# Sample attention: index keys scored inside the projection, the choice begun in the prompt stage, value sets placed between key sets

## What is computed

```
branch A: I[t,s] = sum_h w[t,h] * relu(q_idx[t,h] . k_idx[s]); the 256 best keys per token are kept,
          attention over them (8 query heads, 2 key/value heads)
branch B: blocks of 256 keys; each query head takes its 3 best past blocks by q . mean(k) and its own block
          (8 query heads, 8 key/value heads)
x += (sigmoid(gate_a) * (o_a @ w_br_a) + sigmoid(gate_b) * (o_b @ w_br_b)) @ w_out
```

## Time and profile before

| | us |
|---|---|
| median of 3 runs | 1334.08 (1330.1 to 1346.03) |
| the profiled execution | 1337.45 |
| its span in the trace | 1335.8 |
| around the span | 1.65 |
| projection, up to the first product of the prompt stage | 0 to 216.8 |
| prompt stage, up to the first instruction of the sample stage | 216.8 to 343.3 |
| sample stage: index keys, rows | 343.3 to 400.5 |
| sample stage: B keys and A keys | 400.5 to 520.0 |
| sample stage: B values, rounds | 520.0 to 608.0 |
| sample stage: mask of the choice, A | 608.0 to 663.5 |

### The profile page before, as it was taken

The page is one execution under the profiler, slowest core; times in us unless marked ns, Lnnn a source line. Parts: engine busy times, 40 slices in busy tenths (PEclk is TensorE's granted clock), DMA queues, the critical chain, the costliest instruction groups (busy, mean ns, idle before and its releaser), DMA issues. The chain is left out here.

```text
span 1335.8 us, 14762 instructions
## 1 busy us (share of the span) xinstructions
PE 1011.8 (76%) x5665; PEld 589.9 (44%) x5665; DVE 521.7 (39%) x882; ACT 291.5 (22%) x443; POOL 184.4 (14%) x240
## 2 busy tenths in 40 slices
PE   5999998889679997556679999995077776776720
PEld 4544444667536563112469999452022222222200
DVE  2215885443216979996143330213211111111106
ACT  3112213443136665001100000111001101011102
POOL 4100000000333244331200000000300101011030
PEclk9999998985589999776779999997578889899975
DMA  7212205200377879991584320110299999999963
GB/s 274 80 64 79 81 13 207 83 1 1 95 284 288 342 276 364 383 391 59 179 284 116 95 72 13 48 79 9 82 369 368 376 379 371 372 376 377 367 249 148
DMA packets 149830, 270.20 MB, mean 202 GB/s; under 512 B 18320, under 2 KB 109856, under 8 KB 141584
## 3 DMA queue, kind: packets, MB, share of 16 engines
q1 hardware_dynamic: 126624, 155.59, 34.5%
q0 software_dynamic: 23152, 113.86, 22.6%
HBM read 240.31 MB, written 29.11 MB: 202 GB/s over the span
## 5 line engine op out<-in xcount | busy, mean ns | idle before, releaser
L1853 PE MATMUL bank<-w_gate_up,xT 128*64 128x512 f32 x512 | 131.9, 668 | 47.6 <-DMA w_gate_up<-in_w_e_up 30.8
L637 PE MATMUL bank<-w,hT 128*128 128x512 f32 (+1 forms) x384 | 162.3, 578 | 2.1 <-DMA w<-in_w_in 2.1
L971 PE MATMUL bank<-consts,ring 128*128 128x128 f32 x704 | 95.6, 289 | 20.3 <-ACT kT_s L1144 7.2
L637 PEld LDWEIGHTS bank<-w,hT 128*128 128x128 f32 x384 | 72.6, 194 | 82.4 <-issue 71.3
L971 PEld LDWEIGHTS bank<-consts,ring 128*128 128x128 f32 x704 | 80.6, 147 | 60.3 <-ACT kT_s L1144 34.6
L1144 ACT COPY kT_s<-bank 128x1024 f32<-128x1024 f32 x88 | 86.4, 1016 | 75.9 <-PE bank L971 66.7
L1853 PEld LDWEIGHTS bank<-w_gate_up,xT 128*64 128x64 f32 x512 | 38.9, 152 | 130.4 <-issue 86.0
L1440 PE MATMUL bank<-hT_hi,gate_w_hi 128*128 128x272 f32 x256 | 76.4, 298 | 14.2 <-DVE gate_w_lo L1540 14.2
L1081 PE MATMUL bank<-ring,kT_s 128*32 128x512 f32 (+1 forms) x512 | 56.5, 594 | 37.0 <-DMA ring<-in_cache_v_b,rows_b 29.8
L1440 PE MATMUL bank<-hT_hi,gate_w_lo 128*128 128x272 f32 x256 | 74.8, 292 | 0.0
L1440 PE MATMUL bank<-hT_lo,gate_w_hi 128*128 128x272 f32 x256 | 74.8, 292 | 0.0
(11 more groups left out here) (302 smaller groups left out, 1418.9 us busy)
## 6 DMA issues: line engine op xcount, KB each, us to landing
w_gate_up<-in_w_e_gate SPq DMA_DIRECT2D x64, 512.0 KB, 9.5
w_gate_up<-in_w_e_up SPq DMA_DIRECT2D x64, 512.0 KB, 9.7
w_down<-in_w_e_down SPq DMA_DIRECT2D x32, 1024.0 KB
w<-in_w_in SPq DMA_DIRECT2D x5, 2048.0 KB, 8.3
expert_rows<-zeros SPq DMA_DIRECT2D x17, 512.0 KB, 5.1
gate_w<-in_w_in SPq DMA_DIRECT2D x16, 512.0 KB
expert_rows<-y POOLq DMA_DIRECT2D x16, 512.0 KB, 6.9
w_o<-in_w_out SPq DMA_DIRECT2D x1, 4096.0 KB
```

Source lines behind the costliest of these rows:

```text
L637: last = nc.tensor.matmul(bank[:, n % 4, 0:WID[g]], s.hT[:, k, t * P:(t + 1) * P], w[:, gi % 2, k, 0:WID[g]], start=(k == 0), stop=(k == K ...
L971: last = nc.tensor.transpose(bank[:, u, e * P:(e + 1) * P], ring[:, slot, at:at + P], ident)
L1853: last = nc.tensor.matmul(bank[r, 2, :], xT[:, kk, r], wgu[:, u, part, k, :], start=(kk == 0), stop=(kk == KD - 1))
```

## The change

- The index keys (16 units, `gather_keys`) are gathered during the projection and turned, scored and brought into `row` by steps between items 12 and 28 (`turn_keys`, `score_keys`, `index_rows` on TensorE; `keep_keys`, `keep_row` on ScalarE; `index_keys` on DVE). The gather rows are computed at item 5. For this the projection uses two banks (n % 2) in place of four; its weights, tokens and normalised rows lie in the ring's memory. The query tiles q_a, q_b are filled at the end of the projection.
- The prompt stage runs 8 of the 32 rounds on DVE, a MAX8 after step 1, 5, 9, ..., a MATCH_REPLACE8 after step 3, 7, 11, ...; POOL issues the first two sets of B keys (8 units) at its start.
- The sample stage has 24 rounds. Its sets come in the order of `sample_sets`: the value sets of B stand between key sets. `turn_rows(0)` and six `weigh` calls stand between the key steps, with a buffer `wT` of their own. `spread` comes after the last value set of B.

```diff
+def sample_sets():
+    return [("b", 0, 0), ("b", 0, 1), ("b", 0, 2), ("b", 0, 3), ("b", 1, 0), ("b", 1, 1), ("vb", 0, 0),
+            ("b", 1, 2), ("vb", 0, 1), ("b", 1, 3), ("vb", 0, 2), ("a", 0, 0), ("vb", 0, 3), ("a", 0, 1),
+            ("vb", 1, 0), ("a", 1, 0), ("vb", 1, 1), ("a", 1, 1), ("vb", 1, 2), ("vb", 1, 3),
+            ("va", 0, 0), ("va", 0, 1), ("va", 1, 0), ("va", 1, 1)]
...
 # project, POOL
+                if n == IDX0 - 2:
+                    gather_keys(0)
+                    gather_keys(1)
+                for k in (2, 3):
+                    if n == KEY0 + 3 * (k - 2) + 2:
+                        gather_keys(k)
...
 # project, DVE
+                if n == TT:
+                    gathered_rows()
+                if n == IDX0 + 1:
+                    index_queries()
+                if n == IDX0 + 2:
+                    index_new()
+                if KEY0 < n <= ROW0 and (n - KEY0) % 3 == 0:
+                    index_keys((n - KEY0) // 3 - 1)
...
+            attention_queries()
+            dve.wait_ge(row_done, 5)
...
 # project, TensorE
-                if n >= 4:
-                    pe.wait_ge(nat_ready, n - 3)
+                if n >= 2:
+                    pe.wait_ge(nat_ready, n - 1)
...
+            def index_rows(c):
+                w = 512 if c < 4 else SR
+                pe.wait_ge(key_summed, 2 * len(KSTEPS))
...
+                if KEY0 <= n < ROW0:
+                    k, step = (n - KEY0) // 3, (n - KEY0) % 3
+                    if step < 2:
+                        turn_keys(k, step)
+                    else:
+                        score_keys(k)
+                if ROW0 <= n < ROW0 + 5:
+                    index_rows(n - ROW0)
...
 # prompt, POOL
+            for n, unit in enumerate([(*at, u) for at in sample_sets() for u in range(4)][0:NR]):
+                gather_unit(pool, s, runs, n, unit)
...
 # prompt, DVE, at the end of step m
+                if m < n and m % 2 == 1:
+                    if m % 4 == 1:
+                        link(nc_max(link, s.best8[:, :], s.row[:, :]))
+                    else:
+                        link(nc_replace(link, s.row[:, :], s.best8[:, :]))
...
 # sample
-    UNITS = [("i", g, f, u) for g in range(G) for f in range(2) for u in range(4)]
+    UNITS = [(*at, u) for at in sample_sets() for u in range(4)]
+    TURN_AT = {23: 0, 36: 1}
+    WEIGH_AT = {24: (0, 0), 28: (0, 1), 32: (0, 2), 34: (0, 3), 36: (1, 0), 38: (1, 1)}
...
+            for n in range(1, NS):
+                if n in TURN_AT:
+                    turn_rows(TURN_AT[n], n)
+                if n in WEIGH_AT:
+                    weigh(*WEIGH_AT[n])
+                turn(n)
+                scores(n - 1)
+            scores(NS - 1)
             weigh(1, 2)
+            weigh(1, 3)
+            pe.wait_ge(a_kept, NAR)
             spread(0)
             spread(1)
-            weigh(1, 3)
-            turn_rows(2)
+            turn_rows(2, NS)
...
 # sample, ScalarE
-                if n == NI + 5 * PAIRS:
+                if n == 20:
                     exps(0)
-                if n == NI + NBR * PAIRS + 4:
+                if n == 34:
                     exps(1)
+                if n + 1 in TURN_AT:
+                    keep_turned(TURN_AT[n + 1])
...
 # sample, DVE
             keep_b(0)
+            for r in range(1, NCK):
+                rounds(2)
                 keep_b(r)
+            mask(0)
+            keep_b(NCK)
+            normalise(0)
+            rounds(2)
+            keep_b(NCK + 1)
+            for r in range(NCK + 2, NBR):
+                rounds(3)
+                keep_b(r)
             mask(1)
-            rounds(3)
             normalise(1)
-            rounds(9)
+            rounds(4)
             outputs(0)
-            rounds(TOPK_S // 8 - 24)
+            rounds(TOPK_S // 8 - TP * PAIRS // 2 - 18)
```

More of the change, by code:

```diff
@@ L191, in sa @@
                 return attn.enter_context(nc.sbuf_tensor(name, shape, dt))
[L192 to L193 removed]
+            both = sa("oaT_obT", [P, 2, PAIRS * NTOK])
+            s.oaT, s.obT = (both[:, x, :].rearrange("p (j r) -> p j r", j=PAIRS) for x in range(2))
             with ExitStack() as samp:
@@ L213, in build @@
[L213 to L216, removed]
+                s.q_b, s.q_a = ss("q_b", [P, NB, PAIRS, 32]), ss("q_a", [P, NB, 32])
+                s.row, s.best8 = ss("row", [SR, PAST + SR]), ss("best8_s", [SR, 8])
+                s.ring = ss("ring", [P, NR, SLOT_B * QW])
+                s.lg_i = both[:, :, :].rearrange("p x n -> p (x n)")[:, 0:2 * (PAST + SR)]\
+                    .rearrange("p (g n) -> p g n", g=2)
@@ L244, in project @@
     ROUND0 = IDX0 + 1 + PAIRS
+    G = NB // 4
+    KSTEPS = [(g, f) for g in range(G) for f in range(2)]
+    KEY0 = IDX0 + 2
+    ROW0 = KEY0 + 3 * len(KSTEPS)
     with ExitStack() as ctx:
@@ L457, in index_relu, with keep_keys, keep_row @@
                     .then_inc(relu_done, 1)
+            def keep_keys(k, half):
+                act.wait_ge(key_done, 2 * k + half + 1)
+                if half == 0 and k >= 1:
+                    act.wait_ge(key_scored, k)
+                nc.scalar.copy(kTi[:, 2 * half:2 * half + 2, :], bank[:, 2:4, :]).then_inc(key_kept, 1)
+            def keep_row(c):
+                act.wait_ge(row_done, c + 1)
+                keys = s.row[:, 0:PAST].rearrange("r (f p j e) -> r f e j p", f=2, j=4, e=2)
+                nc.scalar.copy(keys[:, c // 2, c % 2, :, :],
+                               bank[0:SR, 2 + c % 2, :].rearrange("r (j p) -> r j p", j=4)).then_inc(row_kept, 1)
             square(0)
@@ L666, in index_scores, with spread_weights, new_index @@
                 last.then_inc(idx_done, 1)
+            def spread_weights():
+                pe.wait_ge(rot_ready, order[ITEMS.index(("kv", TP))] + 1)
+                for g in range(G):
+                    last = nc.tensor.matmul(bank[:, 2, g * H:(g + 1) * H], const(s, "spread", SR)[:, g * P:(g + 1) * P],
+                                            s.wi[0:SR, TP, :], start=True, stop=True)
+                last.then_inc(w_done, 1)
+            def new_index():
+                pe.wait_ge(q_ready, 1)
+                for b in range(NB):
+                    r = slice(b % 4 * 32, b % 4 * 32 + 32)
+                    last = nc.tensor.matmul(bank[r, 3, b // 4 * SR:(b // 4 + 1) * SR], q_i[0:HD, b, :],
+                                            s.kiT[0:HD, SEQ:NTOK], start=True, stop=True)
+                last.then_inc(new_done, 1)
@@ new lines, in turn_keys @@
+            def turn_keys(k, half):
+                if half:
+                    pe.wait_ge(key_kept, 2 * k + 1)
+                elif k >= 1:
+                    pe.wait_ge(key_summed, 2 * k)
+                else:
+                    pe.wait_ge(new_read, 1)
+                for u in (2 * half, 2 * half + 1):
+                    r = (4 * k + u) % 8
+                    pe.wait_ge(key_in[r], 16 * (k // 2 + 1))
+                    for e in range(4):
+                        last = nc.tensor.transpose(bank[:, 2 + u % 2, e * P:(e + 1) * P], kidx[:, r, e * P:(e + 1) * P],
+                                                   ident)
+                last.then_inc(key_done, 1)
```

403 lines of the change are left out of this document (200 added, 203 removed).

## The result

The changed kernel takes 1345.84 us (median of 20 runs, 1339.33 to 1353.32), the kernel before beside it 1333.24 (20 runs): ratio 1.010, 95% interval 1.0078 to 1.0121. It is one per cent slower, which the forecast (1336, within 2%) counts as no change. The profiled execution has a span of 1343.7 us, 7.9 more than before.

The account below looks back on a forecast made before the run. TensorE bounds the projection, a three-engine loop the prompt stage, TensorE then DMA the sample stage's keys and values. From 1337.45 us, projection +24, prompt stage +24 and sample stage -49 sum to -1: 1336 us, range 1312 to 1361.

Parts of the forecast that it names:

- 7.9 + 4.4 + 7.2 + 2 + 3: Projection: transposes 7.9, scorings 4.4, row products 7.2, short products of weights and new keys 2, wait at index_rows(0) 3.
- Prompt stage, +24 forecast: Prompt stage: sixteen half rounds on DVE add 20 us and a lower clock 4; growth 24, range 17 to 34.
- the replacing ones: Prompt stage: the eight replacing half rounds stick out of gaps by about one us or fit; 4 us taken.
- the clock's term: Prompt stage: with more waits TensorE's clock falls earlier, some 15 us earlier, slowing products; 4 us taken.
- Sample stage, -49 forecast: Sample stage, from its start S: goes from 320.3 to 271 us, a change of -49, range -62 to -33.
- the first weighing: Sample stage: first weighing of B values begins at S + 90, S being the stage's start.
- the mixed stretch: Sample stage, B values among key sets: two pairs 42, four pairs 75, last B set 16 us; end at S + 223.
- The check on the floor of the gathers: Sample stage: 75.5 MB left to gather take 191 us from about S + 20; S + 223 is 12 above it.
- the A end: Sample stage, first spread product to last copy: 55.5 less 5 to 6 for weighing and 2 for waiting, so 48 us.
- The clock rival: Mixed stretch: key steps at 1.2 GHz add 21 us, the prompt stage's clock 6 more; 1363 us, chance 0.18.
- The faster rival: Half rounds cost little (prompt stage's 24 become 6), mixed stretch at the DMA floor, 12 less; 1306 us, chance 0.12.
- The rival in which the choice rules: Sample stage: waits on DVE come to 40, spread starts at S + 225 or later; 1336 to 1346 us, chance 0.1.

Follow-up runs that it names:

- e7_two_banks: The kernel before with only the projection's products in two PSUM banks in place of four; 1332.53 us, ratio 0.9985 to the kernel before.
- e3_keys_first: The changed kernel with its sets in the old order, all key sets ahead of value sets, weighings behind all key steps; 1341.35 us, ratio 1.0096 to the kernel before.
- e1_gap: The changed kernel with the same 16 half rounds of the prompt stage after even steps instead of odd; 1321.20 us, ratio 0.9937 to the kernel before.
- e2_no_prompt_rounds: The changed kernel without half rounds in the prompt stage, all 32 rounds in the sample stage; 1350.96 us, ratio 1.0154 to the kernel before.
- c1_gap_rows: The changed kernel with half rounds after even steps and index-row products one item later; 1315.84 us, ratio 0.9861 to the kernel before.
- e9_gathers_later: The changed kernel with index-key gathers for the third and fourth step issued about two items later; 1339.06 us, ratio 1.0106 to the kernel before.

## Why the prediction was right

**Projection, +24 forecast, +27.2 measured.** The terms were 7.9 + 4.4 + 7.2 + 2 + 3; measured 8.7, 5.2, 7.9, 0.9 and 2.7. That TensorE has no slack there is shown by the doubled transposes (9.3 to 9.7 for 64), that the wait at `index_rows(0)` is real by moving it (2.3 to 4.5 back), and that two banks cost nothing in the kernel before by e7_two_banks. The excess goes with the idle time near 117 us and the slow products behind it: where it is absent, the changed projection ends at 237.8 and 238.6, +21 and +22. It depends on the chip or its conditions, and not on the code alone.

**Prompt stage, +24 forecast, +22.5 measured.** The MAX8 behind `normalise` were to cost 16, the replacing ones 4, the clock 4. Against the stage before, the seven waits for the copy grew by 15.6, TensorE's busy time by 3.6, and its other idle time by 3.3: term for term the forecast. Moving the MAX8 gave 23.0 back, in which the clock's part is contained; that the replacing ones cost anything isn't shown by itself. Against the same kernel without rounds the cost is 27, since the stage before was itself slowed: 126.4 at clock 0.76, and 4.0 less in e7_two_banks, whose prompt stage is the same code, at 0.83. So the clock's term, 4, would have missed against such a profile: it is 11.0 there (113.3 against 102.3). The zero gap and the copy that `turn_out` waits for the earlier trace rows were the right rows to read; DVE's idle share of 58% was not.

**Sample stage, -49 forecast, -41.9 measured.** `spread` came at S + 222.7 where S + 223 was forecast, but that is luck in the steps: the first weighing came at S + 78 and not S + 90, and the mixed stretch took as much longer, 144.6 and not 133. What the runs do show is how little the sum moves: in ten kernels (the changed one among them, two with another order), in all of which DVE had the choice ready and waited 8 to 13 us for `spread`, it lies at S + 220.7 to S + 226.2. The check on the floor of the gathers would explain that, but with a DMA share of 0.80 over the stretch it is an argument and not shown; no run changed the bytes or TensorE's work there. The choice, due at S + 195 to S + 209, was ready at S + 212.4, with 11.21 of waiting at `normalise(1)` (10 to 25 were named). What came on top was DVE's waiting for scores to copy (`keep_b`), 14.57 at 486.71 and 8.77 at 510.44; it left 10.4 and not 14 to 28 of slack. The value sets ahead of these key sets aren't the reason: in e3_keys_first, without them, the choice was ready at S + 213.3.

**The term that was mis-sized is the A end: 48 forecast, 55.6 measured.** The weighing of the last B values is gone from it: from the first `spread` product to the turn is 20.0, was 25.0. The 2 us for the second A value set were not gained: it is there in time, but the third is then waited for (2.05). And the step priced the rest at the clock of the earlier trace rows, and the clock took the gain back: the first turn 3.67 in place of 1.97, and the final products 7.76 from 663.45 to the last copy, before 4.8 (from 658.64). In the three kernels where the clock of this part was at 0.73 the same code took 47.6 to 47.8, the forecast size (e3_keys_first, at 0.75, took 49.5). Why it is 0.61 to 0.75 from kernel to kernel stays open.

The three large terms missed by +3.2, -1.5 and +7.1 us, 8.8 together, of which the A end is 7.6. The forecast also starts from a profiled execution 4.2 above the median of 20 runs of the kernel before (1337.45 against 1333.24): it is a ratio of 0.999, where 1.010 was measured.

**Rivals.** The clock rival (1363) needed key steps at the low level in the mixed stretch; its clock was 0.83 there and not low throughout. The trace does show a set behind a wait of 7.24 taking 4.99 (539.45). The Trainium skill's page "TensorE: Matmul & The Clock Gate", section "HAM oscillation — how this bites in real kernels", says that bursts shorter than the DMA waits between them start slow every time, and the trace agrees: a set without a wait ahead takes 3.62. Sets are slow behind waits shorter than themselves too: 5.34 behind 2.83 at 558.83. But the value sets had time for it, and the turns of key steps between them ran at 1.97, the full-clock time, but for the first after a wait. The faster rival (1306) had a cheap place for the half rounds as its condition; the change doesn't have it, and e1_gap does. The rival in which the choice rules is e2_no_prompt_rounds. The claim that without the prompt's rounds the choice "would come 38 later and rule" was right in kind; it came later by 29.7 at `spread`, since 10.4 of it was slack.

**Where the gain went.** The change took 42 us out of the sample stage. It paid 27 for index keys in a stage where TensorE is full, and 22 to 27 for rounds put where DVE's next work is due at once. Only the second was shown to be avoidable; avoiding it, with the row products one item later, makes c1_gap_rows 1.4% faster than the kernel before, and some 2.4% faster than the change (0.9861 / 1.010).

## What to carry to other kernels

An engine's idle share says nothing of a place: before putting work on it, look at the idle time ahead of the instruction that comes next, and who waits for that one. Eight instructions of 2.3 us cost 23 behind `normalise`, more than their own 18.5 because TensorE's clock was lower as well, and nothing that was seen one step later. Work moved into a stage whose bound engine is full is paid in full. The order of transfers gained nothing here: keys first or mixed, `spread` came within 3 us of the same time.

## What the runs showed of the hardware that was not expected

- The same instruction sequence ran with granted clocks of 0.72 to 0.89 in the prompt stage, 134.5 to 118.8 us, and of 0.61 to 0.73 at the A end, 56.4 to 47.6. Terms of such stages carry that much by themselves.
- TensorE and ScalarE stood still for 3.1 to 3.7 and some 5 us at one place of the projection, in eight profiles of eight on some chips and in none of four on two others. What holds them up stays open; that no event of the core releases them is what the rows show.
- A stage boundary waited until gathers issued shortly ahead of it had landed: 14.42 us in place of 1.81, with the DMA share at 1.0 until some 2.6 us before it opened. That is one profile; the whole time agrees, 9.9 us above e9_gathers_later in the same comparison.
